# Which ScalarE table set is loaded around each norm, and by whom it is asked for

## What the kernel computes

```
def rmsnorm(x, w):
    xf = x.astype(jnp.float32)
    y = xf * lax.rsqrt(jnp.mean(xf * xf, axis=-1, keepdims=True) + EPS)
    return (y * w.astype(jnp.float32)).astype(x.dtype)
...
    g = (y * jax.nn.silu(z.astype(f32))).reshape(b, s, G, SSM_D_INNER // G)
    g = g * lax.rsqrt(jnp.mean(g * g, axis=-1, keepdims=True) + EPS)
```

## Time and profile before

| | |
|---|---|
| median of 3 timed runs | 3477.21 us (3474.63 to 3478.76) |
| span of the profiled execution, first to last instruction | 3482.4 us |
| the profiled execution's own time | not given apart from its span |
| PE busy | 3282.0 us, 94% |
| DVE busy | 1790.9 us, 51% |
| ACT busy | 901.8 us, 26% |
| ACT_TABLE_LOADs in the trace | 57 |

### The profile page before, as it was taken

How to read it: one execution, slowest core, us unless ns; L and a number is a source line. 1 busy time by engine, 2 the same in 40 slices (tenths; PEclk the granted TensorE clock), 3 DMA queues, 4 the chain that set the end, 5 groups by cost and what they waited for, 6 DMA issues and landing times.

```text
span 3482.4 us, 36840 instructions
## 1 busy us (share of the span) xinstructions
PE 3282.0 (94%) x13516; PEld 2085.1 (60%) x13516; DVE 1790.9 (51%) x3363; ACT 901.8 (26%) x1855; POOL 287.3 (8%) x246
## 2 busy tenths in 40 slices
PE   8988989999998989989999999999999899999998
PEld 4743544778744545555555555555544556778887
DVE  2343226777713337777334454444468854554554
ACT  2241212344312221054231131111112523222222
POOL 1200421333101320000000000000000000000000
PEclk9988999999998999999999999999999999999999
DMA  8746876533355972101111212112221021222331
GB/s 271 227 138 204 341 272 214 176 86 97 115 174 202 363 269 61 37 13 41 37 49 39 58 43 66 56 55 61 61 64 58 19 65 45 65 72 80 85 91 61
DMA packets 418494, 394.00 MB, mean 113 GB/s; under 512 B 27888, under 2 KB 353648, under 8 KB 410896
## 3 DMA queue, kind: packets, MB, share of 16 engines
q1 hardware_dynamic: 384768, 348.01, 31.6%
q10 hardware_dynamic: 15120, 23.68, 2.1%
q0 software_dynamic: 18432, 19.98, 1.7%
HBM read 440.78 MB, written 31.52 MB: 136 GB/s over the span
## 4 chain that ended last, share of the span: by engine, by line
PE 61%; DVE 5%; ACT 3%; DMA 2%; issue 1%; ACTq 0%; DVEq 0%; POOL 0%; POOLq 0%
PE psum L716 38%; PE psum L701 6%; PE psum L1204 3%; PE psum L914 2%; DVE arena L2131 2%; PE psum L1290 2%; PE psum L1338 2%; ACT arena L1575 2%; DMA ring<-in_w_branch 1%; PE psum L933 1%; PE psum L1358 1%; PE psum L1370 1%; DVE arena L2128 1%; ACT arena L1567 1%; PE psum L899 1%
## 5 line engine op out<-in xcount | busy, mean ns | idle before, releaser
L716 PE MATMUL psum<-arena,ring 128*128 128x384 f32 (+1 forms) x2592 | 747.2, 439 | 12.8 <-DVE arena L2128 5.3
L716 PEld LDWEIGHTS psum<-arena,ring 128*128 128x128 f32 x2592 | 492.3, 191 | 238.6 <-DVE psum L2128 11.4
L716 PE MATMUL psum<-hT,ring 128*128 128x384 f32 (+1 forms) x2176 | 624.9, 440 | 2.3 <-ACT part_sum L1575 2.2
L716 PEld LDWEIGHTS psum<-hT,ring 128*128 128x128 f32 x2176 | 414.8, 191 | 192.7 <-issue 7.8
L1575 ACT ACTIVATE part_sum<-psum 128x256 f32<-128x256 f32 (+1 forms) x408 | 174.2, 429 | 953.4 <-PE psum L716 808.5
L2128 DVE TENSOR_TENSOR ring<-ring 128x512 f32<-128x512 f32 (+1 forms) x336 | 215.9, 662 | 260.1 <-PE psum L716 257.4
L2128 DVE TENSOR_TENSOR psum<-psum,part_sum 128x256 f32<-128x256 f32 (+1 forms) x328 | 156.2, 479 | 371.5 <-PE psum L716 262.7
L1575 ACT ACTIVATE arena<-psum 128x256 f32<-128x256 f32 (+5 forms) x501 | 210.5, 465 | 506.7 <-PE psum L701 188.8
L701 PE MATMUL psum<-hT,ring 128*128 128x512 f32 (+1 forms) x832 | 314.7, 540 | 14.1 <-DVE hT L2124 11.8
L1567 ACT ACTIVATE arena<-psum,cols 128x256 f32<-128x256 f32 (+3 forms) x280 | 131.7, 493 | 636.0 <-PE psum L914 195.3
L701 PEld LDWEIGHTS psum<-hT,ring 128*128 128x128 f32 x832 | 160.9, 194 | 167.8 <-issue 149.2
(11 more groups left out here) (255 smaller groups left out, 3693.3 us busy)
## 6 DMA issues: line engine op xcount, KB each, us to landing
ring<-in_w_in SPq DMA_DIRECT2D x172, 512.0 KB, 4.1
arena<-in_moe_w SPq DMA_DIRECT2D x44, 1536.0 KB
ring<-in_ada_w SPq DMA_DIRECT2D x96, 512.0 KB, 6.1
ring<-in_w_mod SPq DMA_DIRECT2D x48, 512.0 KB, 5.8
ring<-in_ssm_w_in SPq DMA_DIRECT2D x48, 512.0 KB, 5.5
ring<-in_w_branch SPq DMA_DIRECT2D x64, 256.0 KB, 3.1
hT<-in_moe_w SPq DMA_DIRECT2D x10, 1536.0 KB
ring<-in_moe_w SPq DMA_DIRECT2D x10, 1024.0 KB
```

The lines of the kernel that those rows point to most:

```text
L716: mm = nc.tensor.matmul(flat(bank_, nb), lhs[:, k, :], rhs(k), start=(start and k == 0), stop=(k == kd_ - 1), skip_group_check=True)
```

## The change

`log_table` no longer takes a logarithm of a constant. It asks by name for the one table set that has both logarithm and exponential, and every `inv_root` now calls it first, ahead of its waits, not only those that had `ahead=True`.

```diff
             def log_table():
 
-                act(col("warm"), col("one"), ACT.Ln).then_inc(scalar_done, ac.step())
-
-            def inv_root(name, div, eps, x=True, c=False, ahead=False):
-
-                if ahead:
-                    log_table()
+                nc.scalar.preload_act_table_set("natural_log_exp_and_others")
+
+            def inv_root(name, div, eps, x=True, c=False):
+
+                log_table()
...
-            inv_root("n1_0", D, col("eps"), ahead=True)
+            inv_root("n1_0", D, col("eps"))
```

More of the change, by code:

```diff
@@ L1735, in _ @@
                 squares("n2_0", lambda k: xT[:, k, :], lambda k: (quad_out(3) if k == 6 else None, eng.wait_ge(vector_done, ac.at(("xA", k)))))
-                inv_root("n2_0", D, col("eps"), ahead=True)
+                inv_root("n2_0", D, col("eps"))
             def moe(l):
@@ L1773, in _ @@
                 squares("n1_1", lambda k: xT[:, k, :], lambda k: eng.wait_ge(vector_done, ac.at(("x", "moe0", k))))
-                inv_root("n1_1", D, col("eps"), ahead=True)
+                inv_root("n1_1", D, col("eps"))
                 eng.wait_ge(A_log_landed, ac.at("A_log"))
@@ L1864, in _ @@
                 squares("n2_1", lambda k: xT[:, k, :], lambda k: (quad_out(5) if k == 7 else None, eng.wait_ge(vector_done, ac.at(("xM", k)))))
-                inv_root("n2_1", D, col("eps"), ahead=True)
+                inv_root("n2_1", D, col("eps"))
                 j = jobname("ss", ("b2", 0), "c")
@@ L1934, in _ @@
                     if l:
-                        inv_root(("b2", l), D, col("eps"), c=True, ahead=True)
+                        inv_root(("b2", l), D, col("eps"), c=True)
                     o0 = CONST["rot"][0]
@@ L2110, in _ @@
                 if upto > 7:
-                    inv_root("fin2", D, col("eps"), ahead=True)
+                    inv_root("fin2", D, col("eps"))
             for t in range(4):
```

## The result

The changed kernel took 3456.03 us (median of 4, 3450.97 to 3456.78), the kernel before beside it 3476.11; the ratio is 0.9942, 95% interval 0.9928 to 0.9957, so 20.1 us faster (15 to 25). Over all timed runs, these and the later ones, 94 executions of before have the mean 3474.2 us (standard deviation 4.1) and 20 of the changed kernel 3454.4 (3.6): 19.8 us. One execution of each, of some 8000 us, is left out there.

A forecast was written before the change was run, and what follows sets the result against it. PE bounds the kernel (busy 3282.0 of 3482.4 us), so ACT's time counts only where PE waits. Terms 6.65 + 2.9 + 1.17 + 1.94 - 0.25 = 12.4 us, from median 3477.21 to 3464.8 us; range 3457.5 to 3471.

The forecast's parts named there:

- n1_1: Norm ahead of L1127: lost load and warm logarithm start the exponential earlier, 1.49 us out of PE's 5.10 us wait.
- fin1: Norm behind one of PE's L701 waits for DVE's hT: 1.29 us gained out of a wait of 4.7 us.
- ("b2", 1): Norm behind another of PE's L701 waits for DVE's hT: 1.29 us gained, from a wait little under 4.7 us.
- six state-space waits: PE's six mixer waits at L989 for ACT's partial-sum copy vanish whole: 2.9 us, bounds 0 to 2.9.
- last group: Last state-space group: acs_dram DMA, queued behind the exponential, goes out 1.29 us earlier; PE's 1.17 us wait vanishes.
- layer 1, two norms: Layer 1's last head norm and convolution norm: PE's 0.97 us waits for a copy vanish, 1.94 us.
- second experts: Load ahead of the tangent there: 1.05 us of cover for 1.30 us, so 0.25 us slower.
- the five norms of the chain: Norms whose result PE waits for: the removed load starts each exponential earlier, 4 x 1.29 + 1.49 = 6.65 us.
- the clock rival: Shorter waits at two norms may end before PE's clock falls, 2 us more each: 16.4 us, 3460.8; chance 0.12.
- Only the norms on the chain pay: Elsewhere another engine's sums replace the removed PE waits: only 6.4 us gained, 3470.8 us; chance 0.17.
- The tangents pay: Up to 19 loads ahead of tangents cost 1.30 us each, uncovered: 12.3 us slower, 3489.5 us; chance 0.04.
- A load costs double: A hidden drain gives back up to 1.38 us more at five norms: 19.3 us, 3457.9 us; chance 0.02.

The follow-up runs named there:

- the first two experiments: No edit: the kernel before timed again, 3472.72 us (ratio 0.9993), and the changed kernel again, 3453.26 us (0.9938).
- the groups alone: Kernel before with the one table set asked for only at the eight state-space group norms: 3469.57 us, ratio 0.9988.
- tan_small: Changed kernel with all 21 tangent table loads ahead of the tangents' waits and the small DMA issued before the final norm's squares: 3455.32 us, ratio 0.9948.
- chain_plus4: Kernel before with five table loads instead of one between logarithm and exponential at five norms PE waits for: 3501.74 us, ratio 1.0079.

## Why the prediction was wrong

**Waits, by the terms of the sum.** Means of four traces each, start of product to start of product:

| term | predicted, us | measured |
|---|---|---|
| `n2_0` | 1.29 | 1.25 |
| `n1_1` | 1.49 | 1.46 |
| `fin1`, `("b2", 0)` | 1.29 | 0.82 (0.44 to 1.28) |
| `("b2", 1)` | 1.29 | 1.28 |
| `fin2` | 1.29 | 1.28 |
| six state-space waits | 2.9 | 3.84 |
| last group | 1.17 | 0.59 |
| layer 1, two norms | 1.94 | 2.26 |
| second experts | -0.25 | 0 |
| **sum** | **12.4** | **12.8** |

A wait of layer 1 for a copy fell by another 0.27; it did so in every edited kernel, also where its neighbours were as before, so I don't count it to the change.

- Right: four of the five norms of the chain to 0.04 us, and what would show it (47 loads, 1.39 us, 3.6 us, L989 gone, the tail of `fin2` unchanged at 5.40).
- Of the 1.29 us at `fin1` a third did not come, on the mean. "Nothing stands in for it in these five" was false: the small DMA did, as a wait that was already there, half a microsecond under the one that was removed, and not moved by the change. In the trace of before ACT waited for its landing until 1313.07 and PE started at 1313.53: 0.46 us apart. I had read only the releaser of PE, which was DVE.
- State-space groups and layer 1: the upper bounds were exceeded, because I took the wait from the row. PE's products overlap in the trace (the next starts 0.16 us before the modelled end of the one ahead), so removing a wait shown as 0.39 moves the next product by 0.55, and 0.97 by 1.13. "2.9, the whole wait" was not the whole.
- Last group: half of the bound. The acs DMA did go out earlier, 1.02 us after the logarithm's start instead of 2.02 (943.06 against 941.04 in before), but DVE had it 9.93 us after that instead of 9.29, so PE waited 0.82 us in the first trace instead of 1.17. First the logarithm in before, then the changed kernel:

```profile
941.04 0.69 ACT L1567 ACTIVATE rstd<-psum,cols 128x512 f32<-128x512 f32 x1
```

```profile
928.73 0.69 ACT L1567 ACTIVATE rstd<-psum,cols 128x512 f32<-128x512 f32 x1
...
929.75 0.33 ACTq L1790 DMA_DIRECT2D arena<-acs_dram  x1
...
939.68 1.27 DVE L2124 TENSOR_SCALAR arena<-arena 128x512 f32<-128x512 f32 x4 [4.32 <-DMA arena<-acs_dram]
...
942.50 2.38 PE L1167 MATMUL psum<-arena 128*64 128x512 f32 x16 [0.82 <-DVE arena L2127]
```

- Second experts: the load ran right behind the last copy, 2.5 us ahead of the tangent, since there it is not held by the tangent's wait; in ACT's timeline:

```profile
1106.20 0.60 ACT L1575 ACTIVATE arena<-psum 128x512 f32<-128x512 f32 x1 [0.26 <-PE psum L899]
1106.82 1.28 ACT L1567 ACT_TABLE_LOAD   x1
1110.59 0.37 ACT L1567 ACTIVATE arena<-psum,cols 128x128 f32<-128x128 f32 x1 [2.49 <-PE psum L914]
```

That the two sums agree within 0.4 us is luck in part: `fin1` and the last group brought 1.05 us less than forecast, the state-space waits, layer 1 and the second experts 1.51 more.

**The step that failed is the sum itself: it priced a wait of PE by its length alone.** The products behind a wait often run at the lower clock, and that share was set aside as a rival with the chance 0.12, on the argument that "the shorter wait still reaches past 1312". It does; the clock falls there all the same, but in most traces it comes back after fewer products, and elsewhere it sometimes doesn't fall. Waits give 12.8 us; the measured change is 19.8 on the means. The other 7.0 us are the products themselves, done at the higher clock: over the four traces of each kernel the span fell by 21.5 us on the mean, 12.5 of it idle time of PE and 9.0 busy time, with the same 13516 products (these eight lie a little further apart than the timed runs). The mean clock of the whole span fits that: 0.9763 in before's four traces and 0.9785 in the changed kernel's. At half speed in the low stretches that is 2 x 0.0237 x 3474 = 165 us against 2 x 0.0215 x 3454 = 149 at the lower level. Added up stretch by stretch it is 166 against 148, 18 us less, worth at most 9 where PE was working.

This is not the chance of eight executions, the rival of the first two experiments: every timed run but the first four of before has its granted clock on record. 90 of before have the mean 0.9760 (standard deviation 0.0014), the 20 of the changed kernel 0.9784 (0.0012), which by the same sum is 18 us less at the lower level. So the clock's share belongs to the program.

What in the program brings it is shown in part only. By the granted clock in the traces, 8.5 of the 18 us fewer lie around the shortened waits of `n1_1`, `fin1` and `("b2", 1)`, 6.8 behind the two equal waits of the table, the rest is scattered. At `("b2", 1)` the shorter wait is the cause (six against six); why an equal wait is followed by the lower clock in one program and not in the other stays open.

**The start.** The sum was taken from 3477.21, the median of three runs. Over 94 runs the mean is 3474.2, so 3.0 us come from there. On the means the forecast was 3464.8 - 3454.4 = 10.4 us off: 3.0 by the start, 0.4 by the waits, 7.0 by the clock. The range ended at 3457.5 by the clock rival; it should have reached further down, with the spread of the runs on both kernels in it.

**The rivals.** *Only the norms on the chain pay* is refuted: the groups alone gave 4.2 us, and their waits are gone. *The tangents pay* is refuted by `tan_small`. *A load costs double* is refuted by `chain_plus4` and by the 1.28 us that `("b2", 1)` and `fin2` gave back. *The clock* was the right mechanism at too few places: around its two, `n1_1` and `fin1`, the lower clock takes 6.0 us less on the mean of the four traces, worth at most 3.0 and not 4; it left out `("b2", 1)` and the waits that the change doesn't touch.

## What to carry to other kernels

A ScalarE table load between a logarithm and an exponential is worth its 1.28 us wherever another engine waits for the pair; ask for the one set that has both, early, and check what else the waiting engine waits for at that point, since a second wait half a microsecond below the first takes the gain. Price a wait of TensorE by the distance of product starts, not by the idle time in the row, and then look at the granted clock of the microseconds behind it. On a kernel whose clock falls behind waits, never explain a difference of a few microseconds by one trace against one trace: take the trace of the unchanged kernel a second time first, and compare the granted clock over all timed runs.

## What the runs showed of the hardware

- Executions of one and the same program differed by 14.3 us of span (3482.4 and 3468.1) with the fifteen waits together equal to 0.1 us: PE was busy 3282.0 us in the one and 3265.8 in the other for the same products, at a mean clock of 0.973 and 0.978. The Trainium skill, "TensorE: Matmul & The Clock Gate", section "Part 1: The HAM clock gate", says of the first products of a kernel that the number of slow ones varies from run to run; here it was whole stretches inside the program, as the one from 175 to 195 us, that were low in one execution and not in another.
- A load that the compiler places is held by the next ACTIVATE's wait in the state-space mixer (5.90 us idle ahead of it) and not at the experts (2.49 us idle behind it).
- An equal wait can be followed by different clocks in two programs: the 3.26 us wait was followed by the lower clock in four of four traces of one program and in none of four of the other. Why is open.
